# One row at a time instead of four in the sample's sums of expert rows (hybrid diffusion trunk, one core)

## What is computed

```python
def peer(h, wq, keys, u, v):                       # per block of 128 tokens
    ...                                            # eidx: 128 experts per token, g: their weights
    act = jax.nn.gelu(jnp.einsum('nkd,nd->nk', u[eidx], xb), approximate=False) * g
    return jnp.einsum('nk,nkd->nd', act, v[eidx])
```

## Time and profile before

| | us |
|---|---|
| median of 3 runs | 3951.41 |
| lowest and highest | 3942.88, 3960.61 |
| the profiled execution | 3959.06 |
| its span on the core | 3957.3 |
| busy PE / DVE / POOL | 2632.3 / 2438.0 / 1713.6 |
| mean DMA rate | 272 GB/s |

### The profile page before, as it was taken

How to read it: one execution, slowest core, us unless ns; L and a number is a source line. 1 busy time by engine, 2 the same in 40 slices (tenths; PEclk the granted TensorE clock), 3 DMA queues, 4 the chain that set the end, 5 groups by cost and what they waited for, 6 DMA issues and landing times.

```text
span 3957.3 us, 51649 instructions
## 1 busy us (share of the span) xinstructions
PE 2632.3 (67%) x20431; PEld 1697.2 (43%) x20431; DVE 2438.0 (62%) x5668; ACT 637.6 (16%) x1734; POOL 1713.6 (43%) x1738
## 2 busy tenths in 40 slices
PE   5869678557797457565676776785577951565556
PEld 1868556447685133221543334564576740111111
DVE  4252388897734886645653216898887369667551
ACT  0141212231102022103210001113211021010100
POOL 1000325434410355656565533354344116777774
PEclk8979889668898668877888887896788975767678
DMA  9505669746664889998789987686467639999997
GB/s 341 189 29 194 174 205 325 292 160 228 222 252 159 295 294 328 331 331 323 246 305 355 341 292 189 224 319 249 162 228 272 223 125 346 409 409 409 410 409 295
DMA packets 346465, 1077.34 MB, mean 272 GB/s; under 512 B 30466, under 2 KB 34696, under 8 KB 346096
## 3 DMA queue, kind: packets, MB, share of 16 engines
q0 software_dynamic: 231168, 829.37, 58.6%
q1 hardware_dynamic: 115056, 244.67, 17.1%
HBM read 1070.25 MB, written 3.67 MB: 271 GB/s over the span
## 4 chain that ended last, share of the span: by engine, by line
PE 31%; DVE 25%; DMA 24%; POOL 9%; issue 8%; ACT 2%; DVEq 0%; SPq 0%; ACTq 0%; POOLq 0%
DMA arena<-in_peer_v,arena 15%; POOL arena L2041 8%; DVE arena L2098 5%; PE row_sum L2191 5%; DMA arena<-in_peer_u,arena 4%; PE pair L584 4%; PE pair L1567 4%; DVE row_sum L2111 3%; DMA ring<-in_w_in 3%; PE pair L1580 3%; PE pair L1295 2%; PE pair L1676 2%; DMA ring<-in_w_mod 2%; PE pair L1303 1%; DVE arena L1875 1%
## 5 line engine op out<-in xcount | busy, mean ns | idle before, releaser
L2041 POOL DMA_INDIRECT arena<-in_peer_u,arena x768 | 763.6, 994 | 927.9 <-DVE arena L2098 688.2
L2041 POOL DMA_INDIRECT arena<-in_peer_v,arena x768 | 828.7, 1079 | 668.2 <-DVE row_sum L2111 267.1
L2191 PE MATMUL row_sum<-arena 128*32 128x512 f32 x2048 | 728.2, 795 | 558.6 <-DMA arena<-in_peer_v,arena 446.1
L2098 DVE CUSTOM_DVE_ANT_1 arena<-arena,hT 128x1024 f32<-128x1024 f32 x512 | 621.1, 1222 | 310.8 <-DMA arena<-in_peer_u,arena 305.4
L2191 PEld LDWEIGHTS row_sum<-arena 128*32 128x32 f32 x2048 | 122.3, 127 | 1114.8 <-issue 600.9
L584 PE MATMUL pair<-hT,ring 128*128 128x256 f32 (+1 forms) x2496 | 486.7, 357 | 86.7 <-DVE arena L608 73.4
L584 PEld LDWEIGHTS pair<-hT,ring 128*128 128x128 f32 x2496 | 417.1, 210 | 167.7 <-DVE arena L608 78.7
L2098 DVE CUSTOM_DVE_ANT_0 arena<-arena,pair 128x1024 f32<-128x1024 f32 x256 | 308.4, 1217 | 197.3 <-DMA arena<-in_peer_u,arena 194.1
L2111 DVE SCALAR_TENSOR_TENSOR row_sum<-arena,row_sum 128x1024 f32<-128x1024 f32 x254 | 326.4, 1285 | 33.1 <-DMA arena<-in_peer_v,arena 28.6
L1567 PE MATMUL pair<-hT,ring 128*128 128x128 f32 (+1 forms) x1536 | 267.9, 337 | 21.2 <-DMA ring<-in_w_in 20.6
L1567 PEld LDWEIGHTS pair<-hT,ring 128*128 128x128 f32 x1536 | 240.9, 197 | 56.8 <-DMA ring<-in_w_in 22.5
(11 more groups left out here) (338 smaller groups left out, 3769.8 us busy)
## 6 DMA issues: line engine op xcount, KB each, us to landing
ring<-in_w_in SPq DMA_DIRECT2D x60, 2048.0 KB, 13.9
ring<-in_w_mod SPq DMA_DIRECT2D x24, 2048.0 KB, 9.3
ring<-in_w_br SPq DMA_DIRECT2D x12, 2048.0 KB, 7.9
ring<-in_w_out SPq DMA_DIRECT2D x8, 2048.0 KB, 9.4
ring<-in_peer_wq SPq DMA_DIRECT2D x8, 2048.0 KB, 8.0
arena<-in_peer_u,arena POOLq DMA_INDIRECT x768, 7.6
arena<-in_peer_v,arena POOLq DMA_INDIRECT x768, 8.8
ring<-in_w_in SPq DMA_DIRECT2D x4, 1536.0 KB, 15.6
```

The lines of the kernel that those rows point to most:

```text
L2041: pool.indirect_dma_start(rowbuf[i % NB], None, v_rows if which else u_rows, bass.IndirectOffsetOnAxis(ap=offset, axis=0))\
L2098: nc.vector.tensor_tensor_reduce(row, row, tile_rows(t), 1.0, 0.0, ALU.mult, ALU.add, row_dot[t][:, k:k + 1]).then_inc(sem("u_used"), 1)
L2191: ins = nc.tensor.matmul(row_acc[c][32 * g:32 * g + 32, :], strip[n % 2][:, g, :], rows[g][:, 512 * c:512 * (c + 1)], start=(n == 0), stop ...
```

## The change

In the sample stages a quad is taken apart. A row m has a step of its own, the first at `strip_at`+1, and the strip of its quad is built at `strip_at`. At a step PE does half c = 0 of row m and half c = 1 of row m-1, and then adds one to `v_used`, which now counts rows: row m-1's buffer is free when both its halves are done, and the second of them stands in program order behind the wait for row m. A last step does the second half of row 127. Each v row has its own place in `FETCH`, behind the u row of the same step. `free_at` places the fetch that takes a v row's buffer one step later than that row. The strip of quad n waits until 4n-4 rows of its block are done, which is quad n-2. The prompt's stages keep their order.

```diff
-            def quad_at(t, n):
+            def strip_at(t, n):
                 q, i = divmod(n, 8)
-                return start_at(t, q) + 4 * i + 3
+                return start_at(t, q) + 4 * i
...
-                return m + GROUP + 8 if ON_DVE else quad_at(t, m // 4)
+                return m + GROUP + 8 if ON_DVE else strip_at(t, m // 4) + m % 4 + 1
...
+            def free_at(i):
+                return FETCH[i][0] + (1 if FETCH[i][1] and not ON_DVE else 0)
...
-                    while i < len(FETCH) and (i < NB or FETCH[i - NB][0] <= v):
+                    while i < len(FETCH) and (i < NB or free_at(i - NB) <= v):
...
-                            if v == quad_at(t, n) - 3:
+                            if v == strip_at(t, n):
                                 if 32 * t + n >= 2:
-                                    dve.wait_ge(sem("v_used"), at("v_used", 32 * t + n - 1))
+                                    dve.wait_ge(sem("v_used"), at("v_used", P * t + 4 * n - 4))
...
+            def sum_half(c, m, row):
+                n, g = divmod(m, 4)
+                return nc.tensor.matmul(row_acc[c][32 * g:32 * g + 32, :], strip[n % 2][:, g, :],
+                                        row[:, 512 * c:512 * (c + 1)], start=(n == 0), stop=(n == 31),
+                                        tile_position=(0, 32 * g))
...
-                        for n in range(0 if ON_DVE else 32):
-                            if v == quad_at(t, n):
-                                if n == 0:
+                        for m in range(0 if ON_DVE else P + 1):
+                            if v == (sum_at(t, m) if m < P else sum_at(t, P - 1) + 1):
+                                if m == 0:
                                     pe.wait_ge(sem("peer_res"), at("peer_res", 2 * t))
-                                pe.wait_ge(sem("strip"), at("strip", 32 * t + n + 1))
-                                rows = []
-                                for c in range(2):
-                                    for g in range(4):
-                                        if c == 0:
-                                            rows.append(row_here(pe, 1, t, 4 * n + g))
-                                        ins = nc.tensor.matmul(row_acc[c][32 * g:32 * g + 32, :],
-                                                               strip[n % 2][:, g, :],
-                                                               rows[g][:, 512 * c:512 * (c + 1)],
-                                                               start=(n == 0), stop=(n == 31), tile_position=(0, 32 * g))
-                                ins.then_inc(sem("v_used"), 1)
+                                if m < P:
+                                    if m % 4 == 0:
+                                        pe.wait_ge(sem("strip"), at("strip", 32 * t + m // 4 + 1))
+                                    sum_half(0, m, row_here(pe, 1, t, m))
+                                if m:
+                                    sum_half(1, m - 1, rowbuf[FETCH_NO[1, t, m - 1] % NB]).then_inc(sem("v_used"), 1)
```

More of the change, by code:

```diff
@@ L156, in per_mix @@
     rows = P * nt
-    n.update({"chosen": units, "final_tops": units, "final_exp": units, "u_used": rows, "v_used": rows if p else rows // 4, "strip": rows // 4 * s,
+    n.update({"chosen": units, "final_tops": units, "final_exp": units, "u_used": rows, "v_used": rows, "strip": rows // 4 * s,
               "row_gelu": rows // GROUP, "row_w": rows // GROUP, "no_T": 4 * nt * s, "w_T": 4 * nt * s,
@@ L2017, in row_used @@
                 if which:
-                    eng.wait_ge(sem("v_used"), at("v_used", k + 1 if ON_DVE else 32 * t + k // 4 + 1))
+                    eng.wait_ge(sem("v_used"), at("v_used", P * t + k + 1))
                 else:
@@ L2060, in residual @@
                 def residual(t):
-                    dve.wait_ge(sem("v_used"), at("v_used", P if ON_DVE else 32 * (t + 1)))
+                    dve.wait_ge(sem("v_used"), at("v_used", P * (t + 1)))
                     for c in range(2):
```

## The result

The changed kernel takes 3941.29 us (median of 21 runs, 3932.07 to 3948.59), the one before 3951.41 (21 runs): a ratio of 0.9971, interval 0.9961 to 0.9981. That is 10 us less by the medians, 11 by the ratio, and 36 were forecast. The direction was right, the size was not.

What follows compares the result with a forecast made beforehand. It took a cycle around the v rows to bound sample layer 0 and DMA traffic the last stage. 35 quads at 1.0 us less plus 1 us at the layer's end took 3951.4 us to 3915 us, range 3868 to 3962.

Steps and rivals of the forecast that it cites:

- What bounds the kernel: Sample layer 0: a cycle around the v rows, 529 us of the chain; last stage: DMA traffic at 404 GB/s.
- The clean stretches: Sample layer 0, 2060 to 2223 us and the clean part of 1450 to 1900: 3.5 us a row expected.
- the sum: Sample layer 0's new loop: 10.6 us for three rows, 3.53 a row, 14.1 for four, against 15.1.
- 35 quads: Sample layer 0: the cycle's 529 us at 15.1 us each; 1.0 us less for each, 35 us.
- L: Sample layer 0: time from a v row's start to its landing; taken as 7.8 us, ends 6.2 and 9.7.
- The limit of 380 GB/s: Sample layer 0, mixed rows and weights: no cycle below 12.9 us, so at most 77 us gained.
- The mixer's blocks: Sample layer 0: a 2.05 us projection block may delay a turn; a quarter, 0.5 us, charged per turn.
- The strip: Sample layer 0: DVE builds it with PE three steps behind; its 36.7 us of waits may grow, nothing charged.
- 2223 to 2362 us: End of sample layer 0: no u rows come, weights and norm share the chain; 1 us of gain allowed.
- the 67 us that the scan has in the cycle: Scan, 1900 to 2060 us: the v-row cycle's 42% of the chain there, counted into the 529 us.
- Traffic did not swallow the gain: Rival for sample layer 0: nearly full DMA engines swallow the gain, some 12 us remains, 3940 us; chance 0.27.
- The slower case: Rival for sample layer 0: rows landing after 9.7 us make turns longer, 56 us more, 4007 us; chance 0.12.

Runs made afterwards that it cites:

- e11: Kernel before, quads kept, but both halves of each row summed together as it lands and the row released at once; 3890.4 us, ratio 0.9856 to before.
- e6: Changed kernel with both halves of a row done at its own step, so release does not wait for the next row; 3912.8 us, ratio 0.9905 to before.
- e7: Changed kernel with the 16 quads in retention, preparation and scan taken whole, each row released by itself; 3921.3 us, ratio 0.9921 to before.
- e8: Kernel before with every instruction in place, but buffers released after each row instead of once per quad; 3927.1 us, ratio 0.9937 to before.
- e14: Changed kernel with whole quads, a release for each row, in the scan's steps alone; 3927.1 us, ratio 0.9948 to before.
- e5: Changed kernel with the last row's held second half done before PE turns to mixer work; 3940.4 us, ratio 0.9969 to before.
- e12: Changed kernel with both halves together, u and v rows fetched in fours, and PE's steps two later; 3921.4 us, ratio 0.9928 to before.
- e2: Changed kernel with three strips instead of two, and PE's steps and v fetches two steps later; 3943.8 us, ratio 0.9971 to before.
- e10: Kernel before with quads and a release for each row, but POOL fetching u and v rows by turns; 4129.3 us, ratio 1.0447 to before.
- e13: Changed kernel with both halves at a row's own step and whole quads in retention, preparation and scan; 3898.3 us, ratio 0.9879 to before.

## Why the forecast was wrong

**What bounds the kernel** held. The last stage is the traffic's (722 to 725 us in 14 kernels); layer 0 is a loop round the v buffers, and the gains lie there.

**The clean stretches** came out near the sum, in part by luck. A v row is four records of L2183 or L2191. Counted from 1500 to 1800 us in the kernel before, for L2191 alone (columns as in rows 2, with PE's own two for the engines):

```profile
1500.00:1800.00 300.00, 126.06 (x318) 17.71 (x318) 0.82 0.93 334
```

in the changed kernel, for L2183:

```profile
1500.00:1800.00 300.00, 114.92 (x340) 14.75 (x340) 0.78 0.94 348
```

and in e11, for its line of row sums:

```profile
1500.00:1800.00 300.00, 135.13 (x352) 34.73 (x352) 0.85 0.96 362
```

These are 3.77, 3.53 and 3.41 us a row; 3.78 and 3.53 were the forecast's. (The last 13 and 28 us of the window lie in retention in the two later kernels; up to 1770 us it is 3.76, 3.51 and 3.42.) Projection and gates gained 36 us in the two traces, 15 and 22. The forecast gave 1.0 us to each of 35 quads, the ones that the chain's share of the time made up, and spread them over projection to gates. By PE's records projection and gates alone hold 24 and 12 quads, and the middle 14 more. So 36 quads at 1.0 us are what the two clean stretches gave together, but not each for itself, and both traces have their scatter. The median landing in projection is 6.4 us, and in gates 7.7 instead of 6.3. L was meant for the landings that stand in the chain; in gates those took 8.7 us on average instead of 7.9, so L was 0.9 too low there. The gathers of v rows in the changed kernel, in projection and from 2060 to 2223 us (how many, median us from issue to landing):

```profile
arena<-in_peer_v,arena POOLq DMA_INDIRECT x99, 6.4
...
arena<-in_peer_v,arena POOLq DMA_INDIRECT x46, 7.7
```

The limit of 380 GB/s that the sum put on mixed traffic, worked out from windows of 6 and 7 us, is none: gates carry 365 GB/s in the changed kernel, 374 in e11 and 395 in e6.

**The step that failed** is the count of 35 quads at 1.0 us each, with the parts that should have charged something against it: *The mixer's blocks*, *The strip* ("Nothing is charged") and *2223 to 2362 us*. The forecast priced the mixer from the projection alone and gave the same gain to the 67 us that the scan has in the cycle and to retention and preparation, which lie in its window 1450 to 1900. Rows taken one by one there cost time: the scan lost 10 us where some 4 were to be gained, retention and preparation lost 8, and the rest 4, within the scatter, where 1 us of gain was allowed. e7 puts the price to the test. It is the change with the 16 quads of the middle left whole (each row released by itself, which alone moves the middle by 1 us, 249 before and 248 in e8), and it is 20 us faster than the change and 31 faster than before, near the 36 of the forecast. So 20 of the 26 us that were missing are single rows in the middle, and e14 finds 14 of them in the scan.

Why single rows cost there stays open. It is not the mixer's blocks between a row's halves by themselves (e5 has none and takes as long as the change), nor, by POOL's waits, the held buffer (e5, e12), not the order of the fetches (e12), not the missing strips (e2, e12) and not the number of PE's stops (15 instead of 12). With both halves together the scan gains 7 us, with single rows (e6 against the change) as with quads (e11 against e8); single rows with nothing held still take 105.1 and 105.7 us in retention and preparation (e6, e12), where every kernel with quads there has 97 to 99, but for e10.

**The rivals.** None was it. Traffic did not swallow the gain, since e11 has 57 us in the same stretches. The slower case was built on an L over 8.5; in gates the chain's landings took 8.7, and gates gained 22 us all the same. The loss came in other stretches than the one it was worked out for. The change was right that buffers should be free earlier, and its own pairing of halves takes back part of that, since row m waits for row m+1: e6, without it, has 28 us more.

**What was overlooked** is the largest point. Much of the cost was in the place of one semaphore increment. e8, which moves nothing, gives more than twice what the change gives, and e11, which reorders eight products inside a quad, about five times as much. The forecast named that price (five products after the last landing) and then weighed only the change as it stood.

**The two rules of the Trainium skill.** "DMA: Bandwidth & Descriptors", "Where 436 GB/s comes from", would have left at most 9% in the first window by its 358 GB/s, an estimate; e11 carries 374 GB/s in gates, and the last stage 409. The measurement decides against it for a core that runs alone. Of "TensorEngine Tiling (Array Packing)", "Key Properties", no row shows a cost of its own: e13 has 90 runs of row sums between mixer work where the kernel before has 59, and is 48 us faster. No run here changes the number of runs alone.

## What to carry to other kernels

Where a ring of buffers sets the pace, look first at where in the program each buffer is released, and let each go as soon as its own last reader is done; part of this can be had without moving an instruction, and more by putting a buffer's readers next to each other. Do not tie the release of one buffer to the arrival of the next. Before spreading a batch of work evenly through another engine program, read the stretches of that program one by one: the same spreading gained in two and lost in two others here. A price taken from one stretch does not hold in the next. And a change of this kind is best tried in parts, since a chain of waits names what stands in it and not what it would give to take it out: 66 us of mixer blocks in the chain gave nothing.

## What the runs showed of the hardware

The granted clock of PE in the last stage moved a good deal between kernels with the same products there, and the time of the stage hardly at all. The window from 3400 to 3880 us in the kernel before (columns as in rows 2):

```profile
3400.00:3880.00 480.00, 288.99 (x753) 54.09 (x752) 278.58 (x644) 43.36 (x179) 355.78 (x378) 0.71 1.03 409
```

in the changed kernel:

```profile
3400.00:3880.00 480.00, 324.39 (x780) 36.75 (x780) 269.35 (x599) 43.15 (x178) 354.96 (x378) 0.62 1.03 408
```

and in e6:

```profile
3400.00:3880.00 480.00, 357.31 (x818) 73.40 (x818) 251.99 (x549) 43.14 (x178) 347.07 (x365) 0.98 1.02 405
```

0.71, 0.62 and 0.98 of full speed, and last stages of 723.3, 722.8 and 722.1 us. It is not the order of the products alone that does it. e12 does them in the order of e6, with u and v rows fetched in fours, and e11 too puts both halves of a row together. Their clocks, for 3350 to 3830 us, first e11, then e12:

```profile
3350.00:3830.00 480.00, 291.47 (x775) 92.23 (x771) 265.99 (x605) 43.15 (x178) 357.39 (x379) 0.74 1.03 408
3350.00:3830.00 480.00, 276.50 (x733) 87.31 (x734) 287.39 (x677) 46.77 (x195) 358.03 (x379) 0.76 1.03 409
```

The two kernels with 0.98 (e6 and e13) have both halves together and rows that come one by one; in them PE was busy longest, 347 of these 480 us. I had expected PE at half clock to become the limit of e6 there; since its clock was granted nearly in full, that case did not arise.

Products in different column groups run side by side. A pair in two groups takes 1.04 us (2107.43 in the changed kernel), a pair in one group 1.90 (2095.48 in e11), both with the clock at full. Five products that end a quad take 1.90 us, and all eight of a quad whose rows are there take 1.94 us (e11).
